# Pair sums on VectorE ahead of the norms' column sums, another order of the first loads, and a low part ahead of the bias row

## Chip, cores and metric

The kernel runs on one core of one Trainium2 chip. The metric is the device time of one execution in microseconds (us). TensorE is called PE, VectorE DVE, ScalarE ACT, GpSimd POOL, and SyncE, which here only issues loads, SP.

## What is computed

Two transformer blocks run one after the other on 256 tokens of width 1024, all in float32. The first has an attention mixer with a short convolution and a gated feed-forward part; the second adds 16 meta tokens in front (272 tokens), mixes by a convolution and a linear recurrence, and ends in a layer of 16384 experts, of which each token picks some. The change touches only the norms and the start:

```python
def rms_norm(x, g):
    xf = x.astype(jnp.float32)
    y = xf * lax.rsqrt(jnp.mean(xf * xf, axis=-1, keepdims=True) + RMS_EPS)
    return (y * g.astype(jnp.float32)).astype(x.dtype)

# first_block
h = rms_norm(x, norm_mix_pre[l]);  u = h @ w_in[l]             # norm 0
x = x + rms_norm(y, norm_mix_post[l])                          # norm 1
h = rms_norm(x, norm_ffn_pre[l])                               # norm 2
x = x + rms_norm(y, norm_ffn_post[l])                          # norm 3
# second_block
z = rmsnorm(h, g_mix[l]) @ w_in[l]                             # norm 4, 272 tokens
h = h + peer_ffn(rmsnorm(h, g_ffn[l]), ...)                    # norm 5
```

The attention adds a bias that depends on distance; its rows are made from `rel_bias` by one matrix product, the bias row.

## The kernel before

Activations lie transposed: the 1024 channels are 8 chunks (`KD`) of 128 partitions, the tokens are columns. A weight tile is 128 x 1024 numbers (512 KB), and the kernel streams 424 of them through `ring`, three slots. A product in float32 precision is made of three matmuls: each weight tile is split into a high part `w_hi` (ACT, `split_high`) and a low part `w_lo` (`split_low`: DVE for slots 0 and 1, POOL for slot 2), each activation into `x_hi` (ACT) and `x_lo` (DVE). `project` (L681) then runs 8 x 3 matmuls of 256 or 272 columns for a tile. The order on each engine is written out by hand, and semaphores join the engines. SP loads tile n when the low part of tile n-3 is there (`load_tile`, `low_wait`), so a low part frees a ring slot.

A norm has this order. ACT squares the input in four pairs of chunks into `sq` (`norm_act`, L2129; L2278 for norm 3). PE sums over the channels: one matmul with a matrix of ones for each of the 8 chunks, accumulated in PSUM (`norm_row`, L664, in the trace two records for each matmul). DVE scales and adds epsilon (L1405), ACT takes the root (L2133), DVE the reciprocal (L1408). A norm ahead of a projection goes on with 8 multiplications on DVE (L1414), the high parts on ACT (L2141) and the low parts on DVE (L1427). A norm behind one (1 and 3) scales y in pairs (L1440) and adds it to `hx1` (L1449); norms 2 and 4 square that sum pair by pair as it comes out.

At the start, SP issues the inputs x, the meta tokens, the constants `kept` (with the ones), `first` (constants of later use, with the one-hot matrix of the bias row), `rel`, and then weight tiles. PE first makes the bias row (L703), which needs `first` and `rel`, and then norm 0's sums. DVE copies the bias row out (L1454), and POOL writes it to memory and reads it back spread over 128 partitions (`bias_up`, 1.5 MB, L605); PE needs that at `bias_flip(0)`, after the fourteenth tile of the first projection. The projection starts when DVE raises `in1_even` (L1461).

Of the kernel before, what the change touches and what calls it, by code (L numbers as in the profile page):

```python
# [30 lines left out]
KD = D // P  # L31
TX = 256
N_META = 16
T2 = TX + N_META
TW = KD * P
RING = 3
BODY = 6
# [30 lines left out]
ALU = mybir.AluOpType  # L68
# [58 lines left out]
def bass_transformer_pair(nc, x_t, meta_t, kept, first, second, rel, w1_in, w1_cmp, w1_out, w1_ffn,  # L127
# [3 lines left out]
    with ExitStack() as ctx:  # L131
# [3 lines left out]
        def sem(name):  # L135
            return ctx.enter_context(nc.semaphore(name))
# [6 lines left out]
        hx = sb("hx", [P, KD, T2])  # L143
# [4 lines left out]
        sq = sb("sq", [P, KD, T2])  # L148
# [86 lines left out]
        norm_squares = sem("norm_squares")  # L235
        norm_sums = sem("norm_sums")
# [313 lines left out]
        def _(sp):  # L550
            sp.dma_start(hx1, x_t).then_inc(x_loaded, 16)
            sp.dma_start(hx[:, :, 0:N_META], meta_t).then_inc(meta_loaded, 16)
            sp.dma_start(kept_sb[:], kept).then_inc(param_loaded, 16)
            sp.dma_start(first_sb, first).then_inc(first_loaded, 16)
            sp.dma_start(oh_tab[0:32, :], rel).then_inc(rel_loaded, 16)

            def load_tile(src, n, t, i=None):
                if n >= RING:
                    low_wait(sp, n - RING, i)
                sp.dma_start(ring[:, n % RING, :], src[t]).then_inc(tile_landed[n % RING], 16)  # L560

            for (src, count), b in zip(stream, base):
# [4 lines left out]
                if b == 0:  # L567
                    for t in range(BODY):
                        load_tile(src, t, t)
                    sp.dma_start(second_sb, second).then_inc(second_loaded, 16)  # L570
                    for t in range(BODY, Z1):
                        load_tile(src, t, t)
                        if t % 2 == 0 and t < BODY + 16:
                            j = (t - BODY) // 2
                            sp.dma_start(cmp_w[:, j, :], w1_cmp[j]).then_inc(cmp_loaded, 16)
                    t0 = Z1
# [18 lines left out]
        def _(pool):  # L595
# [3 lines left out]

            pool.wait_ge(brow_ready, 1)  # L600
# [18 lines left out]
            pool_splits(0, B_IN2 + 2)  # L619
# [41 lines left out]
        def _(pe):  # L661
# [7 lines left out]
            def norm_pe(n, width, bank):  # L669
                for k in range(KD):  # L670
                    norm_row(n, k, width, bank)

# [26 lines left out]
            pe.wait_ge(param_loaded, 16)  # L699
            pe.wait_ge(first_loaded, 16)  # L700
# [4 lines left out]


            norm_pe(0, TX, 6)
# [180 lines left out]
            norm_pe(2, TX, 0)  # L888
# [27 lines left out]
            norm_pe(4, T2, 1)  # L916
# [379 lines left out]
            for m in range(16):  # L1296
                slot = tile_split(pe, B_Q + m)
                if m >= BODY:
                    pe.wait_ge(q_copied, m - BODY + 1)
                project(slot, psum[:, m % BODY, 0:TX], TX, first=None if m else X_RAW5).then_inc(tiles_used, 1)  # L1300
                if m == 1:
                    norm_pe(5, TX, 7)
# [90 lines left out]
        def _(dve):  # L1393
# [15 lines left out]

            def norm_pre(n, src, width, bank, gain, done=norm_part):  # L1410
# [19 lines left out]
            def low_norm(s, width):  # L1430
                low_x(s, lambda q: sq[:, 2 * q:2 * q + 2, 0:width])
# [20 lines left out]

            dve.wait_ge(brow_sum, 1)
            dve.tensor_copy(brow[0:N_HEADS, :], psum[0:N_HEADS, 7, :]).then_inc(brow_ready, 1)  # L1454
            dve.wait_ge(param_loaded, 16)
            dve.wait_ge(x_loaded, 16)
            split_low(dve, 0)
            split_low(dve, 1)
            norm_pre(0, hx1, TX, 6, "mix_pre")
            low_norm(X_NORM0, TX)  # L1460
# [118 lines left out]
            norm_post(1, y1, lambda q: y1[:, 2 * q:2 * q + 2, :], TX, 4, "mix_post")  # L1579
            norm_pre(2, hx1, TX, 0, "ffn_pre")  # L1580
# [41 lines left out]
            split_low(dve, B_FFN + 3 * NF + 1)  # L1622
            norm_post(3, y1, ffn_y, TX, 0, "ffn_post")
            dve.tensor_scalar(stay, colv("mu"), -1.0, 1.0, ALU.mult, ALU.add)

            norm_pre(4, hx, T2, 1, "mix2")
# [497 lines left out]
        def _(act):  # L2124
# [23 lines left out]
            split_high(act, 0)  # L2148
            split_high(act, 1)
            norm_root_act(0, TX)  # L2150
# [482 lines left out]
```

## Time and profile before

| | us |
|---|---|
| median of 3 runs | 1609.29 |
| lowest and highest | 1606.79 and 1611.38 |
| the profiled execution's own time | 1603.75 |
| its span, first to last instruction | 1602.0 |
| mean granted clock of PE in it | 0.978 of full |

The profile covers one execution. A group of rows gives start and duration in us from the start of the span, the engine, the line, the operation with the tile written and those read, and the count; what stands in brackets is how long the engine was idle before, and what ended that. The chain of work follows back from the last instruction what each step waited for. In a table of stretches, PEclk is the clock granted to PE, 1.00 being 2.4 GHz and 0.50 being 1.2 GHz.

### The profile page before, as it was taken

The numbers are of one execution on the slowest core, as the hardware profiler recorded it, in microseconds if no ns is written. First come the engines' busy times: TensorE is split into PE (matmuls) and PEld (weight loads), VectorE is DVE, ScalarE is ACT, GpSimd is POOL, SyncE is SP. The second block draws the span as 40 slices with busy tenths as digits, with TensorE's granted clock in tenths as the row PEclk, the third lists the DMA queues.
The fourth block names the chain that finished last, engine by engine and source line by source line (L and its number), as shares of the span: only waits on it lengthen the run. The fifth ranks groups of instructions, "written<-read, shape, count | busy, mean of one in ns | idle before, by whom it ended". The sixth has DMA issues, their size and how long they took to land.

```text
span 1602.0 us, 32178 instructions
## 1 busy us (share of the span) xinstructions
PE 1507.7 (94%) x11588; PEld 1380.9 (86%) x11588; DVE 1082.2 (68%) x1790; ACT 825.8 (52%) x1426; POOL 376.2 (23%) x166
## 2 busy tenths in 40 slices
PE   5998879999789999889999999999999999999998
PEld 4976669999678989889999999999999888888886
DVE  3426457778568988674678997999998544454444
ACT  3335445555455422354466556776665444444444
POOL 1210112222112301012233234221212222222221
PEclk9998999999889999999999999999999999999999
DMA  6630226555324500054645555444444566666664
GB/s 237 234 109 25 66 67 183 180 186 183 106 81 143 164 10 28 15 169 161 184 145 171 182 184 182 148 133 142 138 138 131 183 185 184 194 185 186 184 192 144
DMA packets 66231, 234.86 MB, mean 147 GB/s; under 512 B 8200, under 2 KB 9240, under 8 KB 66160
## 3 DMA queue, kind: packets, MB, share of 16 engines
q1 hardware_dynamic: 65760, 232.31, 45.9%
q0 software_dynamic: 400, 1.59, 0.3%
q8 instruction: 46, 0.75, 0.2%
q14 instruction: 25, 0.20, 0.0%
HBM read 232.80 MB, written 1.06 MB: 146 GB/s over the span
## 4 chain that ended last, share of the span: by engine, by line
PE 72%; DVE 15%; ACT 6%; issue 5%; POOL 1%; DMA 1%; DVEq 0%; SPq 0%; ACTq 0%; POOLq 0%
PE psum L681 35%; PE psum L1372 22%; PE psum L1338 4%; DVE big L1611 3%; DVE w_lo L523 3%; ACT w_hi L509 2%; DVE big L1601 2%; PE psum L1031 2%; DVE big L1651 2%; PE psum L664 1%; ACT big L2187 1%; PE psum L981 1%; PE psum L739 1%; PE psum L1022 1%; PE psum L853 1%
## 5 line engine op out<-in xcount | busy, mean ns | idle before, releaser
L681 PE MATMUL psum<-x_hi,w_hi 128*128 128x256 f32 (+1 forms) x2152 | 624.9, 290 | 39.2 <-DVE x_lo L1427 13.2
L523 POOL TENSOR_TENSOR w_lo<-ring,w_hi 128x1024 fp32r<-128x1024 f32 x141 | 352.7, 2501 | 1117.0 <-ACT w_hi L509 1117.0
L681 PE MATMUL psum<-x_lo,w_hi 128*128 128x256 f32 (+1 forms) x2152 | 613.8, 285 | 0.0
L681 PE MATMUL psum<-x_hi,w_lo 128*128 128x256 f32 (+1 forms) x2152 | 610.3, 284 | 0.0
L509 ACT ACTIVATE w_hi<-ring 128x1024 fp32r<-128x1024 f32 x424 | 445.5, 1051 | 92.0 <-PE psum L681 71.6
L523 DVE TENSOR_TENSOR w_lo<-ring,w_hi 128x1024 fp32r<-128x1024 f32 x283 | 352.2, 1245 | 151.1 <-ACT w_hi L509 147.4
L681 PEld LDWEIGHTS psum<-x_hi,w_hi 128*128 128x128 f32 x2152 | 410.7, 191 | 49.2 <-issue 32.0
L681 PEld LDWEIGHTS psum<-x_hi,w_lo 128*128 128x128 f32 x2152 | 413.4, 192 | 0.0
L681 PEld LDWEIGHTS psum<-x_lo,w_hi 128*128 128x128 f32 x2152 | 411.4, 191 | 1.7 <-issue 1.4
L2095 DVE TENSOR_TENSOR h_lo<-big,h_hi 128x256 fp32r<-128x256 f32 x128 | 69.1, 541 | 163.0 <-ACT h_hi L2519 163.0
L1372 PE MATMUL psum<-w_lo,h_hi 128*128 128x512 f32 x512 | 161.0, 395 | 0.0
L1372 PE MATMUL psum<-w_hi,h_lo 128*128 128x512 f32 x512 | 160.9, 395 | 0.0
L1372 PE MATMUL psum<-w_hi,h_hi 128*128 128x512 f32 x512 | 160.9, 395 | 0.0
L2519 ACT ACTIVATE h_hi<-big 128x256 fp32r (+1 forms) x128 | 53.3, 417 | 184.4 <-PE psum L1372 182.2
L1372 PEld LDWEIGHTS psum<-w_lo,h_hi 128*128 128x128 f32 x512 | 96.0, 187 | 23.6
L1372 PEld LDWEIGHTS psum<-w_hi,h_lo 128*128 128x128 f32 x512 | 96.0, 187 | 23.5
L1372 PEld LDWEIGHTS psum<-w_hi,h_hi 128*128 128x128 f32 x512 | 95.9, 187 | 23.4
L2494 ACT ACTIVATE sq<-kept_sb,sq 128x128 f32<-128x128 bf16 x256 | 83.6, 400 | 2.5 <-PE psum L1338 2.0
L1651 DVE SCALAR_TENSOR_TENSOR big<-big 128x272 f32<-128x272 f32 x120 | 70.8, 640 | 0.3
L2470 ACT ACTIVATE big<-psum 128x256 f32 (+1 forms) x68 | 26.2, 385 | 76.9 <-PE psum L681 76.8
L2503 ACT ACTIVATE psum<-psum 128x256 f32<-128x256 f32 x60 | 22.1, 368 | 66.3 <-PE psum L681 66.0
L695 PE MATMUL psum<-h_hi,w_hi 128*128 128x256 f32 x176 | 51.1, 291 | 3.5 <-DVE h_lo L1615 2.8
(315 smaller groups left out, 1738.0 us busy)
## 6 DMA issues: line engine op xcount, KB each, us to landing
ring<-experts SPq DMA_DIRECT2D x256, 512.0 KB, 3.5
ring<-w_ffn SPq DMA_DIRECT2D x66, 512.0 KB, 3.5
ring<-w_in SPq DMA_DIRECT2D x46, 512.0 KB, 3.6
ring<-w_mid SPq DMA_DIRECT2D x24, 512.0 KB, 3.5
ring<-w_out SPq DMA_DIRECT2D x16, 512.0 KB, 3.6
ring<-w_q SPq DMA_DIRECT2D x16, 512.0 KB, 3.9
big<-w_cmp SPq DMA_DIRECT2D x8, 512.0 KB, 5.1
big<-bias_rows POOLq DMA_DIRECT2D x1, 1536.0 KB, 9.2
```

Of the source, the lines that this page charges most:

```text
L509: act.activation(w_hi[:, n % RING, :], ring[:, n % RING, :], ACT.Copy).then_inc(high_ready, 1)
L523: eng.tensor_tensor(w_lo[:, n % RING, :], ring[:, n % RING, :], w_hi[:, n % RING, :].bitcast(F32), ALU.subtract).then_inc(low_ready2 if n ...
L681: mm = pe.matmul(dst, w[:, slot, k * P:(k + 1) * P], x[:, k, t0:t0 + width], start=(n == 0), stop=(n == 3 * len(chunks) - 1))
L695: mm = pe.matmul(psum[:, 4 + m // 2, (m % 2) * TX:(m % 2 + 1) * TX], w[:, slot, m * P:(m + 1) * P], h[:, par, :], start=False, stop=False, ...
L1031: mm = pe.matmul(psum[0:nt, FULL[name][hh], c:c + r.shape[1]], gram[hh][0:nt, a, h, 0:nt], r, start=True, stop=True)
L1338: mm = pe.matmul(gate_bank(q)[:, :, t], hot_1[q % 2][:, t, :].bitcast(F32), hot_2[q % 2][:, t, :], start=True, stop=True)
L1372: mm = pe.matmul(psum[:, 4 + 2 * tt + half, :], h[:, par, tt * P:(tt + 1) * P], w[:, slot, half * 512:(half + 1) * 512], start=False, stop ...
L1611: dve.tensor_tensor(ffn_h[:, par, :], ffn_g[:, par, :], ffn_c[:, par, 1, :], ALU.mult).then_inc(ffn_whole, 1)
L1651: ins = dve.scalar_tensor_tensor(out=conv_y[:, m, :], in0=glu[:, m, t:t + T2], scalar=w, in1=conv_y[:, m, :], op0=ALU.mult, op1=ALU.add)
L2095: dve.tensor_tensor(h_lo[:, e % 2, :], act_all[:, trip(e, i, per), :], h_hi[:, e % 2, :].bitcast(F32), ALU.subtract).then_inc(coef_low, 1)
L2494: ins = act.activation(hot_2[q % 2][:, t, :], hit_2[q % 2][:, :, t], ACT.Copy, scale=chosen_t[:, 0, bass.ds(at, 1)])
L2519: act.activation(h_hi[:, e % 2, :], act_all[:, trip(e, i), :], ACT.Copy).then_inc(coef_high, 1)
```

## The change

Four things change.

- `fold_pair(n, q, width)` on DVE adds the squares of chunk 2q+1 to those of chunk 2q, and PE sums four such pairs instead of eight chunks. Norms 0 and 3 fold all four pairs; norms 2 and 4 fold only pairs 2 and 3, and keep four single chunks. Norms 1 and 5 stay as they are.
- SP loads x, `kept`, tile 0, `first`, `rel`, tiles 1 and 2, and then the meta tokens, which stood second.
- PE makes norm 0's sums before the bias row. DVE splits only tile 0 ahead of norm 0, and copies the bias row out after the low parts of x and of tile 1. ACT makes the high part of tile 1 behind norm 0's root.
- POOL makes the low part of tile 2 before it writes the bias row out.

```diff
@@ SP
             sp.dma_start(hx1, x_t).then_inc(x_loaded, 16)
-            sp.dma_start(hx[:, :, 0:N_META], meta_t).then_inc(meta_loaded, 16)
             sp.dma_start(kept_sb[:], kept).then_inc(param_loaded, 16)
-            sp.dma_start(first_sb, first).then_inc(first_loaded, 16)
-            sp.dma_start(oh_tab[0:32, :], rel).then_inc(rel_loaded, 16)
...
+            load_tile(w1_in, 0, 0)
+            sp.dma_start(first_sb, first).then_inc(first_loaded, 16)
+            sp.dma_start(oh_tab[0:32, :], rel).then_inc(rel_loaded, 16)
...
-                    for t in range(BODY):
+                    for t in range(1, BODY):
                         load_tile(src, t, t)
+                        if t == 2:
+                            sp.dma_start(hx[:, :, 0:N_META], meta_t).then_inc(meta_loaded, 16)
@@ POOL
             pool.memset(oh_tab[32:33, :], NEG).then_inc(neg_row, 1)
+            pool.wait_ge(neg_row, 1)
+            split_low(pool, 2, None, (2,))
             pool.wait_ge(brow_ready, 1)
             pool.dma_start(bias_rows, brow[0:N_HEADS, :]).then_inc(brow_stored, 16)
...
-            pool_splits(0, B_IN2 + 2)
+            pool_splits(3, B_IN2 + 2)
@@ PE
-            def norm_pe(n, width, bank):
-                for k in range(KD):
+            def norm_pe(n, width, bank, rows=0):
+                for k in range(rows):
                     norm_row(n, k, width, bank)
+                for q in range(rows // 2, 4):
+                    pe.wait_ge(norm_folded, FOLDED[n] + q - rows // 2 + 1)
+                    mm = pe.matmul(psum[:, bank, 0:width], const("ones"), sq[:, 2 * q, 0:width], start=(q == 0), stop=(q == 3))
+                    if q == 3:
+                        mm.then_inc(norm_sums, 1)
...
             pe.wait_ge(param_loaded, 16)
+            norm_pe(0, TX, 6)
             pe.wait_ge(first_loaded, 16)
...
-            norm_pe(0, TX, 6)
...
-            norm_pe(2, TX, 0)
+            norm_pe(2, TX, 0, 4)
...
-            norm_pe(4, T2, 1)
+            norm_pe(4, T2, 1, 4)
...
-                    norm_pe(5, TX, 7)
+                    norm_pe(5, TX, 7, 8)
@@ DVE
+            def fold_pair(n, q, width):
+                dve.wait_ge(norm_squares, KD * n + 2 * q + 2)
+                dve.tensor_tensor(sq[:, 2 * q, 0:width], sq[:, 2 * q, 0:width], sq[:, 2 * q + 1, 0:width],
+                                  ALU.add).then_inc(norm_folded, 1)
...
+            for q in range(4):
+                fold_pair(0, q, TX)
+            split_low(dve, 0)
+            dve.wait_ge(param_loaded, 16)
+            dve.wait_ge(x_loaded, 16)
+            norm_pre(0, hx1, TX, 6, "mix_pre")
+            low_norm(X_NORM0, TX)
+            split_low(dve, 1)
             dve.wait_ge(brow_sum, 1)
             dve.tensor_copy(brow[0:N_HEADS, :], psum[0:N_HEADS, 7, :]).then_inc(brow_ready, 1)
-            dve.wait_ge(param_loaded, 16)
-            dve.wait_ge(x_loaded, 16)
-            split_low(dve, 0)
-            split_low(dve, 1)
-            norm_pre(0, hx1, TX, 6, "mix_pre")
-            low_norm(X_NORM0, TX)
             dve.sem_inc(in1_even, 3)
...
+            for q in range(4):
+                fold_pair(3, q, TX)
             norm_post(3, y1, ffn_y, TX, 0, "ffn_post")
@@ ACT
             split_high(act, 0)
+            norm_root_act(0, TX)
             split_high(act, 1)
-            norm_root_act(0, TX)
             high_norm(X_NORM0, 0, TX)
```

The folds of norms 2 and 4 stand as `for q in (2, 3): fold_pair(n, q, width)` right before their `norm_pre`. The rows below show the order on two engines. In brackets stand the semaphores that a row waits for.

PE at the start of the program, before: `psum<-big` is the bias row, `psum<-sq,kept_sb` a sum of squares, and L681 the first projection.

```order
L660 UNCONDITIONAL_BRANCH [waits barrier_Pool_Activation_PE_DVE_SP_release]
L703 MATMUL psum<-big 8x512 [waits rel_loaded,neg_row,first_loaded,param_loaded]
L664 MATMUL psum<-sq,kept_sb 128x256 [waits norm_squares] x8
L771 UNCONDITIONAL_BRANCH
L771 ISA
L711 ISA [waits low_ready]
L681 MATMUL psum<-x_hi,w_hi 128x256 [waits x_split,in1_even]
```

PE at the same place of the change, where L693 is the projection.

```order
L667 UNCONDITIONAL_BRANCH [waits barrier_Pool_Activation_PE_DVE_SP_release]
L681 MATMUL psum<-sq,kept_sb 128x256 [waits norm_folded,param_loaded]
L681 MATMUL psum<-sq,kept_sb 128x256 [waits norm_folded] x3
L716 MATMUL psum<-big 8x512 [waits neg_row,rel_loaded,first_loaded]
L781 UNCONDITIONAL_BRANCH
L781 ISA
L721 ISA [waits low_ready]
L693 MATMUL psum<-x_hi,w_hi 128x256 [waits x_split,in1_even]
```

The eight sums became four, wait for the folds, and stand ahead of the bias row.

DVE at the start, before: the copy of the bias row, two low parts of weights, the norm, the low parts of x.

```order
L1454 COPY big<-psum 8x512 [waits brow_sum]
L523 TENSOR_TENSOR w_lo<-ring,w_hi 128x1024 [waits high_ready,x_loaded,param_loaded]
L523 TENSOR_TENSOR w_lo<-ring,w_hi 128x1024 [waits high_ready]
L1405 TENSOR_SCALAR rms<-psum 128x256 [waits norm_sums]
L1408 RECIPROCAL rms<-rms 128x256 [waits norm_root]
L1414 SCALAR_TENSOR_TENSOR sq<-hx,kept_sb,rms 128x256 [waits dve_step]
L1414 SCALAR_TENSOR_TENSOR sq<-hx,kept_sb,rms 128x256 x7
L1427 TENSOR_TENSOR x_lo<-sq,x_hi 128x2x256 [waits high_part] x4
```

DVE at the same place of the change, with the folds (L1422) first.

```order
L1422 TENSOR_TENSOR sq<-sq 128x256 [waits norm_squares] x4
L525 TENSOR_TENSOR w_lo<-ring,w_hi 128x1024 [waits high_ready]
L1415 TENSOR_SCALAR rms<-psum 128x256 [waits norm_sums,x_loaded,param_loaded]
L1418 RECIPROCAL rms<-rms 128x256 [waits norm_root]
L1429 SCALAR_TENSOR_TENSOR sq<-hx,kept_sb,rms 128x256 [waits dve_step]
L1429 SCALAR_TENSOR_TENSOR sq<-hx,kept_sb,rms 128x256 x7
L1442 TENSOR_TENSOR x_lo<-sq,x_hi 128x2x256 [waits high_part] x4
L525 TENSOR_TENSOR w_lo<-ring,w_hi 128x1024 [waits high_ready]
L1477 COPY big<-psum 8x512 [waits brow_sum]
```

The second low part and the copy moved behind the low parts of x, and both stand ahead of the `sem_inc` of `in1_even`, which is no row of its own.

## Rows read from the trace of the kernel before

**Rows 1.** The page: span, and busy time of PE with its share.

```profile
span 1602.0 us, 32178 instructions
PE   1507.7 (94%) x11588; PEld 1380.9 (86%) x11588; DVE 1082.2 (68%) x1790; ACT 825.8 (52%) x1426; POOL 376.2 (23%) x166
```

**Rows 2.** Chain of work, 0 to 120 us: start, duration, what.

```profile
4.32 6.29 DMA big<-rel
...
10.85 1.86 PE psum L703 x2
12.71 5.17 PE psum L664 x16
...
24.64 39.45 PE psum L681 x312
```

**Rows 3.** Timeline, 0 to 75 us, rows of several engines.

```profile
2.17 1.63 SPq L553 DMA_DIRECT2D kept_sb<-kept  x1
...
8.28 2.19 ACT L2129 ACTIVATE sq<-hx 128x512 f32<-128x512 f32 x4
...
11.73 1.06 ACT L509 ACTIVATE w_hi<-ring 128x1024 fp32r<-128x1024 f32 x1 [1.26 <-DMA ring<-w_in]
...
13.36 2.34 DVE L523 TENSOR_TENSOR w_lo<-ring,w_hi 128x1024 fp32r<-128x1024 f32 x2
...
14.09 1.28 ACT L2133 ACT_TABLE_LOAD   x1
...
17.91 0.42 DVE L1405 TENSOR_SCALAR rms<-psum 128x256 f32<-128x256 f32 x1 [2.21 <-PE psum L664]
...
23.78 2.49 DVE L1427 TENSOR_TENSOR x_lo<-sq,x_hi 128x512 fp32r<-128x512 f32 x4
...
24.64 0.58 PE L681 MATMUL psum<-x_hi,w_hi 128*128 128x256 f32 x1 [6.77 <-DVEq L1461]
...
25.55 2.94 POOL L523 TENSOR_TENSOR w_lo<-ring,w_hi 128x1024 fp32r<-128x1024 f32 x1 [8.61 <-ACT w_hi L509]
```

**Rows 4.** Single microseconds: length, busy time by engine, PEclk, DMA share, GB/s.

```profile
22.00:23.00 1.00, 0.00 (x0) 0.00 (x0) 1.00 (x4) 0.78 (x2) 0.00 (x0) 0.78 0.97 359
29.00:30.00 1.00, 1.00 (x9) 1.00 (x8) 0.00 (x0) 0.11 (x1) 0.00 (x0) 0.81 0.46 74
432.00:433.00 1.00, 0.01 (x1) 0.02 (x1) 1.00 (x3) 0.66 (x1) 0.00 (x0) 0.58 0.00 0
438.00:439.00 1.00, 1.00 (x3) 0.68 (x3) 0.00 (x0) 0.00 (x0) 0.00 (x0) 0.51 0.00 0
```

**Rows 5.** Loads by line: KB each, us from issue to landing.

```profile
big<-bias_rows POOLq DMA_DIRECT2D x1, 1536.0 KB, 9.2
hx<-x_t SPq DMA_DIRECT2D x1, 1024.0 KB, 6.2
...
kept_sb<-kept SPq DMA_DIRECT2D x1, 539.0 KB, 6.5
```

**Rows 6.** Timeline: the load of tile 7 (first of two), and its high part.

```profile
35.45 4.02 SPq L560 DMA_DIRECT2D ring<-w_in  x2
41.30 1.06 ACT L509 ACTIVATE w_hi<-ring 128x1024 fp32r<-128x1024 f32 x1 [1.43 <-PE psum L681]
```

**Rows 7.** Timeline of norm 2's last sums and last squares.

```profile
216.87 1.99 PE L664 MATMUL psum<-sq,kept_sb 128*128 128x256 f32 x8 [0.26 <-ACT sq L2129]
216.97 0.63 ACT L2129 ACTIVATE sq<-hx 128x512 f32<-128x512 f32 x1 [0.16 <-DVE hx L1449]
```

**Rows 8.** Timeline from the last feed-forward step through norms 3 and 4.

```profile
417.71 0.43 DVE L1615 TENSOR_TENSOR h_lo<-big,h_hi 128x256 fp32r<-128x256 f32 x1 [0.48 <-ACT h_hi L2268]
...
422.98 2.06 ACT L2278 ACTIVATE sq<-psum 128x512 f32<-128x512 f32 x4 [4.35 <-PE psum L695]
423.63 3.72 PE L664 MATMUL psum<-sq,kept_sb 128*128 128x256 f32 x16 [0.75 <-ACT sq L2278]
...
432.99 6.88 PE L664 MATMUL psum<-sq,kept_sb 128*128 128x272 f32 x16 [5.63 <-ACT sq L2129]
...
435.04 1.45 ACT L2129 ACTIVATE sq<-hx 128x544 f32<-128x544 f32 x2 [0.73 <-DVE hx L1449]
```

More of the change, by code:

```diff
@@ L235, in bass_transformer_pair @@
         norm_squares = sem("norm_squares")
+        norm_folded = sem("norm_folded")
+        FOLDED = {0: 0, 2: 4, 3: 6, 4: 10}
         norm_sums = sem("norm_sums")
@@ L1579, in _ @@
             norm_post(1, y1, lambda q: y1[:, 2 * q:2 * q + 2, :], TX, 4, "mix_post")
+            for q in (2, 3):
+                fold_pair(2, q, TX)
             norm_pre(2, hx1, TX, 0, "ffn_pre")
@@ L1622, in _ @@
             split_low(dve, B_FFN + 3 * NF + 1)
+            for q in range(4):
+                fold_pair(3, q, TX)
             norm_post(3, y1, ffn_y, TX, 0, "ffn_post")
             dve.tensor_scalar(stay, colv("mu"), -1.0, 1.0, ALU.mult, ALU.add)
+            for q in (2, 3):
+                fold_pair(4, q, T2)
             norm_pre(4, hx, T2, 1, "mix2")
```

## The prediction

> **What bounds the kernel now.** I read the page first. PE is busy 94% of a span of 1602.0 us [rows 1], so what a change can win outside the matmuls is small. The question is which stretches have PE short of work, and what the chain runs through there. The chain of work from 0 to 120 us shows the first: it waits for the load of `rel` until 10.61, then takes 1.86 us for the bias row, 5.17 us for norm 0's sums, and reaches the projection at 24.64 [rows 2]. From there on PE is the chain for 39 us. So whatever comes earlier ahead of 24.64 moves everything behind it. The timeline of the same stretch shows what stood ready: ACT had squared x by 10.47 (8.28 + 2.19), while the sums began only at 12.7 and the scaling at 17.91 [rows 3]. In norms 3 and 4 the sums are again a piece of the chain in which everything else waits (3.72 and 6.88 us), and in norm 2 their last part (1.99 us) [rows 7, 8].
>
> **What one sum costs.** The clock comes first. Norm 2's last four matmuls took 1.99 us, norm 3's eight 3.72 us [rows 7, 8]: (3.72 - 1.99)/4 = 0.43 us each, and 1.99 - 4 x 0.43 = 0.27 us of tail. PEclk was full in both. At 1.2 GHz I take twice the spacing, 0.86, and a tail of 0.4 (estimate); norm 4's eight in 6.88 us, at 1.2 GHz until just before 439 [rows 4, 8], and the bias row's 512 columns in 1.86 us [rows 2] agree with it. A fold is a DVE addition of 128x256 f32. None of this form is in the trace; the nearest is the subtraction of 128x256 at L1615, 0.43 us [rows 8]. As a bound from above, a quarter of the 1024 columns of L523, whose two took 2.34 us, is 0.29, so the fixed part is already in 0.43; the range is 0.3 to 0.5, and I take 0.43 and 0.05 for each handover.
>
> **Norm 0.** The squares stay at 8.28 to 10.47, a pair each 0.55 us, since the load of x stays first. Folds then end at about 9.35, 9.9, 10.4 and 10.95. PE needs `kept` too, which landed at 2.17 + 6.5 = 8.7 [rows 3, 5] and now stands a place further ahead. PE starts cold at 9.4, so its four sums come every 0.86 us, more slowly than the folds: 9.4 + 4 x 0.86 + 0.4 = 13.25. Before, scaling began at 17.91 [rows 3]. That is 4.65 us earlier. Three things could be later than 13.25. DVE splits tile 0 ahead of the scaling: tile 0 was the sixth load and its high part began at 11.73; now it is third, ahead of 690 KB of `first`. At the 1024 KB + 539 KB landed by 8.7, 512 KB more at the same pace is 9.7 to 10.5, so ACT starts on it when it is done with the squares at 10.5, ends at 11.55 (1.06), DVE at 12.75 (2.34/2) [rows 3]. ACT's table load of 1.28 us then fits in 11.6 to 12.9. If the tile lands as late as before, DVE ends at 14.0 and 0.75 us of gain is lost. The bias row now follows the sums at 13.3 to 15.1, off the chain.
>
> **From scaling to projection** it was 24.64 - 17.91 = 6.73 us [rows 3], and the same instructions follow. ACT's high part of tile 1 (1.06 us) goes into ACT's idle time between root and the first `x_hi`, during DVE's reciprocal and first multiplications. New is that a low part of 1.2 us and the bias row's copy of 0.7 us stand ahead of the `sem_inc` that lets PE go. In the trace PE was let go at 24.6 by DVE's sequencer while the last low parts of x ran until 26.27 [rows 3]: the increment passes work that is only queued. So I price this at 0.1 us for two more instructions to issue. If the increment had to wait until the copy is done, it would cost 26.27 + 1.2 + 0.7 - 24.6 = 3.6 us; that is the upper bound. The Trainium skill (TensorE: Matmul & The Clock Gate, its opening table) gives ScalarE, VectorE and GpSimdE queues that hold 8 instructions, strictly in order. By it the five queued here (three low parts of x, one of the tile, the copy) fit; no row shows five. I keep 0.1. The low part of tile 1 ends at 22.8, the second tile's matmuls start near 25 (24.64 + 4.8 - 4.55): hidden. Tile 2's low part on POOL keeps its place behind ACT (25.55 before, near 21 now [rows 3]); the DMA pair of the bias row goes behind it. Norm 0's term is 4.65 - 0.1 = **4.55 us**.
>
> **Norm 2.** The last squares end at 217.60 (216.97 + 0.63), the sums at 218.86 [rows 7]. With folds the last one ends at 218.08, its sum at 218.12 + 0.70 = 218.82. That is **0.0 us** (bounds -0.3 to 0.2): the two matmuls saved are paid by a fold in the chain.
>
> **Norm 3.** Squares start at 422.98 and end at 425.04, one each 0.49 us [rows 8]. DVE is idle. The last fold ends at 425.51, the last sum at 425.56 + 0.70 = 426.26, against 427.35. That is **1.1 us** (bounds 0.9 to 1.3).
>
> **Norm 4.** PE starts at 432.99 at 1.2 GHz and is the bound, since the squares are there at 436.49 (435.04 + 1.45) [rows 8]. Now it has four chunks and two pairs of 272 columns, 0.91 each: 6 x 0.91 + 0.4 = 5.85 us; the folds (last by 437.0) are in time for the fifth and sixth, which start at 436.6 and 437.5. Against 6.88 that is **1.0 us**. Had the clock been low throughout, eight took 7.7 and the gain were 1.85; had it been full, the last sum hangs on the last square and the gain is 0.
>
> **Sum.** 4.55 + 0.0 + 1.1 + 1.0 = 6.65, say 6.7 us. Span 1602.0 becomes 1595.3, the profiled execution's 1603.75 becomes 1597.1. This execution lies 5.5 us under the median of the runs, so the median becomes 1609.3 - 6.7 = 1602.6. What follows norm 4 is unchanged. A run of this kernel can tell about 0.3% (4.8 us) from no change, so the forecast lies only 1.9 us beyond that.
>
> **Rivals.**
> - *The clock is still up when the projection starts* (chance 0.12). Before, PE was idle from 17.88 to 24.64, the clock fell in the second from 22 (0.78, so about 4.7 us in), and the projection ran at 1.2 GHz until about 29.4 [rows 4]. Ahead of norm 4 it fell at 432.16, 4.8 us after norm 3's sums. Now PE works until 15.1 and starts again near 20.1, an idle of 5.0 us instead of 6.8. Should the clock rise in 9.4 to 15.1 and hold, the first 24 matmuls come each 0.12 instead of 0.21 us: up to 2.3 us more, a gain of 9.0, 1600.3 us. The Trainium skill (same page, "HAM oscillation") has the clock fall after a gap without matmuls, so a shorter gap speaks for this rival; the trace agrees with the rule, falling in both gaps above, but the cooler, shorter work ahead of the gap speaks against it.
> - *The gate of the projection, or a late tile 0* (0.14). The increment waits for part of the queue (up to 3.6 us), or the first tile costs 0.75. The gain is 3 to 5.5: 1604 to 1606.3 us.
> - *The spread bias rows meet the tile stream* (0.12). Their 1.5 MB took 9.2 us [rows 5] in a quiet time from 16 to 25; now they are issued near 26.5, when tiles 6 and 7 and other loads of 512 KB are under way. Tile 7 was issued at 35.45 and its high part needed it at 41.30 [rows 6], 5.8 us for a load that takes about 4 alone. 1.5 MB at 400 GB/s is 3.9 us of traffic. Two tiles late by 2 us cost at most some 3 us, and ACT makes high parts ahead of need: the gain is 3.5 to 6, 1603.3 to 1605.8.
> - *Slower* (0.04). By the same mechanism: if the spread load's packets keep the stream waiting for its whole 9.2 us and again in the next slots. A stall beyond 6.7 us turns the sign, 11.5 us gives slower by 0.3% (1614). It decides from the point where tile 7 lands more than 6.7 us after PE could use it; its slack makes that unlikely.
> - *The change doesn't do what it says* (0.05): norm 0's chain is set by another wait, for instance the folds or `kept`, and gains under 3 us: 1605 to 1607.5.
>
> **How the numbers follow.** The forecast has 0.53 and its own range 1601 to 1604.5. The range 1599 to 1606.5 takes in the warm clock below and most of the gate, tile stream and norm 4 at full clock above. Faster by over 0.3% (under 1604.5): 0.49 of the forecast, 0.12 of the first rival and 0.07 of the next two, 0.68 in all. Slower 0.04, and 0.28 between.
>
> **What would show it.** In the new profile: the first sum near 9.4 and scaling near 13.3; the projection 6.8 us behind, let go by DVE's sequencer; no ACT high part waiting for `ring` from 25 to 45; norm 3's scaling 4.4 us behind its first square before, 3.3 now; norm 4's sums of some 5.9 us at 1.2 GHz. Wrong would make it a scaling in norm 0 that waits for the low part of tile 0 or for a slow load, a projection that starts after the copy of the bias row, or clock phases that fall otherwise.

## The result, and the profile after

The changed kernel takes 1594.43 us (median of 4 runs, 1593.44 to 1597.27), the kernel before beside it 1608.04 (4 runs, 1604.76 to 1611.38): a ratio of 0.9922 with a 95% interval of 0.9901 to 0.9943, so faster by 12.5 us (by the medians 13.6). The forecast was 6.7 us. The profiled execution of the changed kernel took 1597.27 us, its span is 1595.2; before it was 1603.75 and 1602.0. **Between the two traces lie 6.8 us, as forecast; between the runs lie 12.5 to 13.6.** That difference is what the experiments are about. The agreement of the traces with the forecast is in part luck, as the leads at the end of this section show.

The page of the changed kernel, span and busy time:

```profile
span 1595.2 us, 32113 instructions
PE 1508.6 (95%) x11564; PEld 1380.9 (87%) x11564; DVE 1087.6 (68%) x1802; ACT 826.0 (52%) x1426; POOL 376.9 (24%) x166
```

The chain of work of the changed kernel at its start (start, us, what), to be held against [rows 2]:

```profile
0.75 5.72 DMA hx<-x_t
...
8.49 0.44 DVE sq L1422
...
9.07 3.77 PE psum L681 x8
...
19.72 39.67 PE psum L693 x312
```

The load of `rel` and the bias row are gone from the chain; it goes from x by its squares and one fold to the sums. The projection's first thirteen tiles run without a pause again (39.67 us for 312 matmuls, 39.45 before [rows 2]), so no load stalls them. The timeline of the same stretch, against [rows 3]:

```profile
7.83 2.19 ACT L2152 ACTIVATE sq<-hx 128x512 f32<-128x512 f32 x4
8.49 1.99 DVE L1422 TENSOR_TENSOR sq<-sq 128x256 f32<-128x256 f32 x4 [8.49 <-ACT sq L2152]
9.07 3.75 PE L681 MATMUL psum<-sq,kept_sb 128*128 128x256 f32 x8 [9.07 <-DVE sq L1422]
9.93 1.04 ACT L511 ACTIVATE w_hi<-ring 128x1024 fp32r<-128x1024 f32 x1
...
11.00 1.23 DVE L525 TENSOR_TENSOR w_lo<-ring,w_hi 128x1024 fp32r<-128x1024 f32 x1 [0.52 <-ACT w_hi L511]
...
12.75 1.87 PE L716 MATMUL psum<-big 33*8 33x512 f32 x2
12.97 0.42 DVE L1415 TENSOR_SCALAR rms<-psum 128x256 f32<-128x256 f32 x1 [0.74 <-PE psum L681]
...
18.84 2.49 DVE L1442 TENSOR_TENSOR x_lo<-sq,x_hi 128x512 fp32r<-128x512 f32 x4
...
19.72 0.58 PE L693 MATMUL psum<-x_hi,w_hi 128*128 128x256 f32 x1 [5.09 <-DVEq L1478]
...
20.69 4.02 POOL L525 TENSOR_TENSOR w_lo<-ring,w_hi 128x1024 fp32r<-128x1024 f32 x1 [19.58 <-ACT w_hi L511]
...
21.25 1.22 DVE L525 TENSOR_TENSOR w_lo<-ring,w_hi 128x1024 fp32r<-128x1024 f32 x1
...
22.39 0.67 DVE L1477 COPY big<-psum 8x512 f32<-8x512 f32 x1
...
24.99 0.28 PE L693 MATMUL psum<-x_hi,w_hi 128*128 128x256 f32 x1
25.10 0.28 PE L693 MATMUL psum<-x_lo,w_hi 128*128 128x256 f32 x1
...
29.11 0.94 POOL L612 DMA_DIRECT2D big<-bias_rows  x1 [3.76 <-DMA bias_rows<-big]
```

PE waits for DVE's first fold of two squares (8.49) and sums from 9.07 on, at 1.2 GHz. Norm 0's scaling stands at 12.97 instead of 17.91 and the projection 6.75 us behind it at 19.72 instead of 24.64: 4.92 us earlier. It starts while the low part of tile 1 and the copy of the bias row (22.39) are still queued on DVE. Its matmuls start 0.2 us apart until 24.99 and 0.12 apart from then: full clock comes 5.3 us into the projection. Two things took longer and cost nothing: POOL's low part (4.02 us, 2.94 before [rows 3]) and its wait for the stored bias rows (3.76).

Norms 3 and 4 of the changed kernel, against [rows 8]:

```profile
420.42 2.07 ACT L2301 ACTIVATE sq<-psum 128x512 f32<-128x512 f32 x4 [5.21 <-PE psum L707]
421.05 1.89 DVE L1422 TENSOR_TENSOR sq<-sq 128x256 f32<-128x256 f32 x4 [4.59 <-ACT sq L2301]
421.53 2.17 PE L681 MATMUL psum<-sq,kept_sb 128*128 128x256 f32 x8 [1.21 <-DVE sq L1422]
...
429.33 3.99 PE L671 MATMUL psum<-sq,kept_sb 128*128 128x272 f32 x8 [5.63 <-ACT sq L2152]
...
433.12 1.79 PE L681 MATMUL psum<-sq,kept_sb 128*128 128x272 f32 x4
```

Last, the places at which each kernel scales in norms 1 to 4, and three high parts of weight tiles that both make (number 25, 133 and 421 of the 424). The kernel before, on its timeline:

```profile
116.58 1.04 ACT L509 ACTIVATE w_hi<-ring 128x1024 fp32r<-128x1024 f32 x1
...
208.18 0.42 DVE L1405 TENSOR_SCALAR rms<-psum 128x256 f32<-128x256 f32 x1 [1.59 <-PE psum L664]
...
218.90 0.42 DVE L1405 TENSOR_SCALAR rms<-psum 128x256 f32<-128x256 f32 x1 [2.02 <-PE psum L664]
...
427.39 0.42 DVE L1405 TENSOR_SCALAR rms<-psum 128x256 f32<-128x256 f32 x1 [7.50 <-PE psum L664]
...
439.90 0.44 DVE L1405 TENSOR_SCALAR rms<-psum 128x272 f32<-128x272 f32 x1 [4.08 <-PE psum L664]
...
649.82 1.05 ACT L509 ACTIVATE w_hi<-ring 128x1024 fp32r<-128x1024 f32 x1
...
1577.63 1.04 ACT L509 ACTIVATE w_hi<-ring 128x1024 fp32r<-128x1024 f32 x1
```

The changed kernel:

```profile
110.30 1.04 ACT L511 ACTIVATE w_hi<-ring 128x1024 fp32r<-128x1024 f32 x1
...
205.63 0.42 DVE L1415 TENSOR_SCALAR rms<-psum 128x256 f32<-128x256 f32 x1 [1.59 <-PE psum L671]
...
216.30 0.42 DVE L1415 TENSOR_SCALAR rms<-psum 128x256 f32<-128x256 f32 x1 [0.79 <-PE psum L681]
...
423.74 0.42 DVE L1415 TENSOR_SCALAR rms<-psum 128x256 f32<-128x256 f32 x1 [0.79 <-PE psum L681]
...
434.95 0.44 DVE L1415 TENSOR_SCALAR rms<-psum 128x272 f32<-128x272 f32 x1 [1.64 <-PE psum L681]
...
640.08 1.05 ACT L511 ACTIVATE w_hi<-ring 128x1024 fp32r<-128x1024 f32 x1
...
1570.87 1.04 ACT L511 ACTIVATE w_hi<-ring 128x1024 fp32r<-128x1024 f32 x1
```

The lead of the changed kernel is 4.9 us at the projection, 6.3 at the 25th tile, 2.6 at norms 1 and 2, 3.7 at norm 3, 5.0 at norm 4, 9.7 at the 133rd tile and 6.8 at the end. Only three of these steps lie where instructions differ: the start (4.9), norm 3 (1.1) and norm 4 (1.3), 7.3 us in all. The other steps, where the instructions are the same, are -2.4 us up to norm 1, 4.8 between norm 4 and the 133rd tile and -3.0 from there to the 421st. They nearly cancel in this pair of traces, and so the two traces come out 6.8 us apart. Between 110 and 208, and from 450 to 720, the same instructions run in the same order, and the lead moves by 3.0 to 4.8 us at a time. The tables of stretches (length, busy us of PE, PEld, DVE, ACT, POOL, then PEclk, DMA share and GB/s) say with what. Before, then changed:

```profile
116.00:200.00 84.00, 70.74 (x410) 52.95 (x411) 48.91 (x105) 45.52 (x143) 4.78 (x2) 0.92 0.14 44
600.00:660.00 60.00, 55.85 (x1023) 52.76 (x1022) 47.29 (x92) 16.34 (x35) 6.27 (x2) 0.94 0.06 20
660.00:735.00 75.00, 66.28 (x628) 62.58 (x623) 49.93 (x69) 35.35 (x45) 14.53 (x6) 1.00 0.41 133
```

```profile
116.00:200.00 84.00, 74.48 (x385) 56.73 (x385) 44.90 (x97) 43.95 (x141) 5.18 (x3) 0.84 0.14 42
600.00:660.00 60.00, 56.60 (x1035) 53.53 (x1032) 47.72 (x97) 16.48 (x35) 6.27 (x2) 1.00 0.04 11
660.00:735.00 75.00, 66.55 (x508) 63.55 (x508) 46.27 (x56) 36.10 (x45) 15.93 (x7) 0.93 0.48 154
```

In the attention stage (116 to 200), where PE waits for ACT and DVE again and again, the changed kernel's execution had a mean clock of 0.84 against 0.92; around 600 to 660 it is the other way round (1.00 against 0.94), and from 660 the other way again. So a single trace holds some microseconds that belong to where the clock stood in that one execution; the stretch behind norm 4 is compared over all traces at the end of the experiments.

### The profile page after: what moved, and what is told of

Same layout as the page of the kernel before. It is cut to its first block, busy times and chain, and to the rows that moved or that the text cites. A ratio compares the mean times of both kernels' runs of the same rounds, so it can differ in the third digit from the quotient of the medians.

```text
span 1595.2 us, 32113 instructions
## 1 busy us (share of the span) xinstructions
PE 1508.6 (95%) x11564; PEld 1380.9 (87%) x11564; DVE 1087.6 (68%) x1802; ACT 826.0 (52%) x1426; POOL 376.9 (24%) x166
## 4 chain that ended last, share of the span: by engine, by line
PE 73%; DVE 16%; ACT 5%; issue 5%; POOL 1%; DMA 0%; DVEq 0%; ACTq 0%; POOLq 0%
PE psum L693 36%; PE psum L1382 22%; PE psum L1348 4%; DVE big L1630 3%; DVE w_lo L525 3%; DVE big L1674 2%; ACT w_hi L511 2%; DVE big L1620 2%; PE psum L1041 1%; PE psum L749 1%; PE psum L991 1%; PE psum L863 1%; PE psum L671 1%; DVE sq L1429 1%; POOL w_lo L525 1%
## 5 line engine op out<-in xcount | busy, mean ns | idle before, releaser
L693 PE MATMUL psum<-x_hi,w_hi 128*128 128x256 f32 (+1 forms) x2152 | 627.1, 291 | 37.4 <-DVE x_lo L1442 12.9
L693 PE MATMUL psum<-x_lo,w_hi 128*128 128x256 f32 (+1 forms) x2152 | 615.8, 286 | 0.0
L693 PE MATMUL psum<-x_hi,w_lo 128*128 128x256 f32 (+1 forms) x2152 | 612.2, 284 | 0.0
L693 PEld LDWEIGHTS psum<-x_hi,w_hi 128*128 128x128 f32 x2152 | 412.7, 192 | 48.9 <-issue 31.7
L693 PEld LDWEIGHTS psum<-x_hi,w_lo 128*128 128x128 f32 x2152 | 415.6, 193 | 0.0
L693 PEld LDWEIGHTS psum<-x_lo,w_hi 128*128 128x128 f32 x2152 | 413.7, 192 | 1.7 <-issue 1.4
```

The source lines that it names most:

```text
L693: mm = pe.matmul(dst, w[:, slot, k * P:(k + 1) * P], x[:, k, t0:t0 + width], start=(n == 0), stop=(n == 3 * len(chunks) - 1))
```

## The experiments

All gains are given by the ratio to the kernel before on the same chip, times 1607 us; ranges are the 95% intervals. The theory at the start: the chain loses 6.8 us, and the rest of the 12.5 is PE's clock, which the two traced executions do not represent. The rivals: one part of the change is worth more than its chain shows, or the medians were a chance. The chain's worth of a part is what its traces win at the projection and in the norms.

**One part at a time.** The whole change again, the start alone (`norm_pe(2|3|4, ..., 8)` and the folds of norms 2 to 4 out), the pair sums of norms 2 to 4 alone (norm 0, order and loads as before), and the kernel before once more.

> The whole change once more, for a second trace and more runs. Theory A (the sum holds, and the profiled execution of before was a lucky one while the rest of the 13.6 us is chance of where the clock falls): over more runs the gain comes down to 7 to 9 us. Theory B (something beyond the shortened chain pieces gains in every run): the gain stays at 12 to 14 us, and the same pieces of the chain are 6 us shorter than in the trace of before in a place that the sum did not name. Both expect scaling in norm 0 near 13.0 and the projection near 19.7.

> Only the start of the change (loads, norm 0 with pair sums ahead of the bias row, tile 2's low part first); norms 2, 3 and 4 sum eight chunks as before. Theory A: 4.9 us faster than before, as the projection starts 4.9 us earlier. Theory B, if the unnamed gain belongs to the start: 10 to 12 us faster.

> Only the pair sums of norms 2, 3 and 4, with the start as before. Theory A: 2.4 us faster (0, 1.1 and 1.3 us). Theory B, if the unnamed gain belongs to the folds: 7 to 9 us faster. If both halves gain as Theory A says but the whole gains 13, the two parts act on each other.

> The kernel before, unchanged, for a second trace of it and as a test of what the comparison tells from nothing. Both theories: a ratio of 1.000 within 0.002. Theory A expects its trace to have the same length as the first trace in all stretches in which the clock is up, and other lengths only where PE works at 1.2 GHz; its span then is 1602 plus what it spends more at 1.2 GHz. Theory B expects a stretch in which it is longer at full clock too.

Measured: the whole 12.9 us (10.9 to 14.9; 1594.27 us, 5 runs), the start 7.7 (5.1 to 10.3), the pair sums 5.6 (3.9 to 7.4), the kernel before -0.5 (-1.9 to 1.0). The gain is no chance: the 7 to 9 us of Theory A for the whole did not come. The parts add up (13.3), and each is worth more than its chain, 4.9 and 2.4, and less than Theory B gave it. Within one kernel the time goes with PE's mean granted clock: of the six runs of the start alone, 1595.49 and 1595.58 us stand at 0.982, 1603.60 and 1606.46 at 0.974. The second trace of the kernel before (1604.84 us) takes 208.45 us from norm 2's scaling to norm 3's for 208.49 in the first; elsewhere it has other low stretches and other lengths, as Theory A expected. The trace of the second execution of the whole change shows how much the clock moves for one and the same program:

```profile
12.50 1.02 PE L716 MATMUL psum<-big 33*8 33x512 f32 x2
19.46 0.58 PE L693 MATMUL psum<-x_hi,w_hi 128*128 128x256 f32 x1 [5.94 <-DVEq L1478]
...
22.57 0.28 PE L693 MATMUL psum<-x_hi,w_lo 128*128 128x256 f32 x1
...
116.00:200.00 84.00, 74.43 (x365) 55.58 (x364) 43.58 (x92) 40.81 (x130) 4.76 (x2) 0.80 0.11 38
```

The bias row took 1.02 us instead of 1.87, full clock came 3.1 us into the projection instead of 5.3, and then the attention stage ran at 0.80: it reached that stage 2.0 us ahead of the first execution (108.01 and 110.04), and norm 1 2.1 us behind it (207.70 and 205.63).

**The clock held up.** In both kernels PE gets idle matmuls in its gaps, on a bank that nobody reads: 11 ahead of the projections of norms 0, 2 and 4, 5 ahead of the last `ffn_down` and 9 between norms 3 and 4.

```diff
+            def fill_gap(norm, part, bank):
+                filler(4, bank)
+                pe.wait_ge(norm_root, norm + 1)
+                filler(3, bank)
+                for q, n in enumerate((2, 1, 1)):
+                    pe.wait_ge(norm_part, 4 * part + q + 1)
+                    filler(n, bank)
```

> The kernel before with idle matmuls (zeros times constants, 0.43 us each at 2.4 GHz, into a bank nobody reads) in PE's gaps: 11 each between the sums and the projection in norms 0, 2 and 4, 9 between norms 3 and 4, 5 ahead of the last down tile. The output is not touched. Theory C (the gain beyond the traced one is the clock: in most executions norms 3 and 4 meet PE at 1.2 GHz, where eight sums cost twice): the clock stays up through the gaps, the projections start at 2.4 GHz, and this kernel is 5 to 9 us faster than before. Theory D (the surplus is not the clock): little changes, -3 to +3 us.

> The whole change with the same idle matmuls. Against the run of the kernel before with them, Theory C expects only the shortened chain at full clock: 4.9 us at the start, 1.1 in norm 3, nothing in norms 2 and 4, 6 us in all. Theory D expects the full 12.6 us between these two as well. If the clock is what costs, this is also the fastest kernel: 1585 to 1591 us.

Measured: 1591.11 us (5 runs) for the kernel before with them, 14.6 us faster (12.5 to 16.7) for 5 to 9 expected, and 1588.10 (5 runs) for the changed one, 16.1 faster (13.5 to 18.6). **With the clock held up the change is worth 3.0 us by the medians and 1.4 by the ratios**, not 12.5, though the projection still starts 5.0 us earlier (24.87 and 19.86). Two of the changed kernel's five runs stand apart (1593.95 and 1592.19 us, clock 0.981 and 0.983; the others 1586.09 to 1588.10 at 0.986 to 0.988), so this worth is known to some 4 us either way: it is less than 12.5, and not clearly less than the chain's 6. Norm 4 and the start of the projection, of the kernel before with idle matmuls:

```profile
24.87 0.39 PE L681 MATMUL psum<-x_hi,w_hi 128*128 128x256 f32 x1 [0.82 <-DVEq L1482]
...
428.92 2.10 PE L664 MATMUL psum<-sq,kept_sb 128*128 128x272 f32 x8 [0.20 <-ACT sq L2150]
...
116.00:200.00 84.00, 74.36 (x399) 56.51 (x398) 46.18 (x99) 44.24 (x141) 5.65 (x3) 0.86 0.14 48
```

and of the changed kernel with them:

```profile
19.86 0.39 PE L693 MATMUL psum<-x_hi,w_hi 128*128 128x256 f32 x1 [0.83 <-DVEq L1499]
20.08 0.28 PE L693 MATMUL psum<-x_lo,w_hi 128*128 128x256 f32 x1
...
427.01 1.52 PE L681 MATMUL psum<-sq,kept_sb 128*128 128x272 f32 x4 [0.68 <-DVE sq L1443]
...
116.00:200.00 84.00, 74.88 (x391) 57.28 (x391) 43.50 (x92) 42.92 (x135) 6.84 (x3) 0.84 0.15 45
```

The projection now starts at full clock (0.12 us from the second matmul on). Norm 4's sums hang on the last square in both, end at 431.02 (428.92 + 2.10) and 428.53 (427.01 + 1.52), and nothing is gained there: from the first sum (426.16 and 423.78) it is 4.86 and 4.75 us. Norm 3's pair sums win there what they won without: the lead is 1.2 us at norm 2, 2.4 at norm 3, 2.5 at norm 4 and 2.8 at the end. The attention stage, which has no idle matmuls, stays at 0.84 to 0.86.

The granted clock says how the 14.6 us come about. In the stretches that it gives as 1.2 GHz, PE worked 53.7 and 64.0 us in the two traces of the kernel before, and 32.1 us with the idle matmuls. Work at 1.2 GHz takes twice as long, so 22 to 32 us less of it should give 11 to 16 us (an estimate). The two traces of the changed kernel have 60.0 and 64.6 us of it, 35.6 with the idle matmuls: over the whole execution they show no better clock than the kernel before.

**The parts with the clock held up.** The start alone and the pair sums alone, with the same idle matmuls.

> The start alone (loads, order, pair sums of norm 0), with the idle matmuls that hold the clock up ahead of the projections. The kernel before with the same idle matmuls took 1591.1 us, the whole change with them 1588.1. Theory A (the surplus of the start over its 4.9 us of chain is the clock in and around the gaps): the start gains at most its chain, 3 to 5 us, 1586 to 1588. Theory B (the start's 7.7 us belong to the part itself, whatever the clock does): 1583.5. Theory C (the attention stage takes back part of any earlier start, as the two traces with idle matmuls show): 1588 to 1589.5.

> The pair sums of norms 2, 3 and 4 alone, with the same idle matmuls; against 1591.1 us for the kernel before with them. Theory A: with the clock up, norm 2 gives 0, norm 3 1.1 us as without them and norm 4 some 0.4, since its last sum hangs on the last square: 1589.5. Theory B (the folds' 5.6 us belong to them whatever the clock does): 1585.5. Theory C (nothing here is behind the attention stage, so it takes nothing back): as A.

Measured: 1589.52 us (6 runs), 16.9 faster than before (12.9 to 20.7), and 1593.61 (6 runs), 14.9 (11.4 to 18.5). Against the filled kernel before (14.6) the start is worth 2.2 us and the pair sums 0.3, where they were worth 7.7 and 5.6. Each comparison has 4 us or more to either side, so no single one is firm; all three stand at or under their chain, and none shows its surplus. Theory A is nearest for both parts, and Theory C (the attention stage takes part back) fits the start as well.

**More idle matmuls**, 23 in the attention stage too:

> The whole change with the idle matmuls of before and 23 more in the attention stage: 10, 2 and 7 ahead of the first three turns of the probabilities, into the bank that the turn then overwrites, and 4 ahead of the output projection. In the traces that stage took 71 to 81 us, the same matmuls at other clocks. If it is the clock, the stage takes 71 us or less, the spread of the runs shrinks, and the time falls below the filled kernel's 1588.1, to 1580 to 1586. If the stage's length has another cause, the time stays or rises by the 10 us of matmuls put in.

Measured 1589.49 us (5 runs), 17.5 faster (15.4 to 19.6). The clock of 116 to 200 rises to 0.94, but from the 25th tile to norm 1's scaling it takes 95.4 us as before (95.2 with the idle matmuls in the norms alone), and the kernel is not faster. The 1580 to 1586 us of the clock's theory did not come. That the idle matmuls stand in the way of real ones would explain both; it was not measured by itself.

**The start taken apart.** The new order without pair sums in any norm, and the whole change with the old order of loads:

> Only the order of the start: loads, norm 0 ahead of the bias row, tile 2's low part first; norm 0 sums eight chunks, and so do norms 2 to 4. Eight sums from about 8.6 us on, mostly at 0.86 us each, end near 15.2 to 15.6. By the chain it gains 2.3 to 2.8 us in its trace, and the pair sums of norm 0 are worth the other 2.2. Theory D, with the surplus in the order of the loads: it gains 5 us or more.

> The whole change but the order of the loads, which is that of before (meta tokens second, the constants of later use and rel ahead of tile 0). Tile 0's high part then starts at 11.7 as before, its low part ends near 14.0, and scaling in norm 0 waits for it: 1.0 us slower than the whole change. If the surplus lies in the loads (Theory D), it is 4 us slower or more.

Measured: the order alone 2.7 us (1.0 to 4.3; 12 runs), for a projection 3.8 us earlier (20.88), where 2.3 to 2.8 were expected; the whole change with the old loads 8.5 (6.1 to 11.1), for a projection at 20.68. So by the chain the order, loads included, gives 3.8 us, the folds of norm 0 some 1.1 more, and the loads 1.0 of all this. The times part it otherwise: norm 0's folds are worth 5.0 us (7.7 for the start less 2.7), and the loads 4.4 (12.9 less 8.5), which meets the 4 us at which Theory D put the surplus into the loads; but the order alone, with the new loads, stays under the 5 us that the same theory asked of it. Each of these differences has about 3 us to either side.

**Delays.** One, two and three needless additions of 1.1 us each on DVE, between norm 0's multiplications and the low parts of x, in the changed kernel and then in the one before; and norm 3's pair sums alone. The first of the additions:

```diff
             norm_pre(0, hx1, TX, 6, "mix_pre")
+            dve.tensor_tensor(conv_m, hx1[:, 0:4, :], hx1[:, 4:8, :], ALU.add)
             low_norm(X_NORM0, TX)
```

> The whole change with one needless DVE addition of 128x1024 (about 1.13 us) into an unused region, between norm 0's multiplications and the low parts of x, so that everything from the first projection on comes 1.1 us later. Theory E (the untraced surplus is where the clock's falls meet the attention stage, and that place is nearly the same in each execution): the time changes by something else than 1.1 us, between -4 and +8 us. Theory F (the clock falls at random places, so only the mean over executions counts): 1.1 us slower than the whole change, within the noise of 1 us: 1595.4.

> The same with two such additions, 2.3 us. Theory E: a change that is not 2.3 us, and not twice that of one addition. Theory F: 2.3 us slower than the whole change, 1596.5.

> The same with three, 3.4 us. Theory E: back near the whole change plus 3.4 us, 1597.7, with one or both of the other two off the line between. Theory F: 1597.7 as well, with the other two on the line.

> The kernel before with one needless DVE addition (1.1 us) between norm 0's multiplications and the low parts of x. Theory G (most executions of the kernel before fall at an unlucky place of the clock, and any shift helps): less than 1.1 us slower, or faster, by as much as 4 us. Theory H (its place is an ordinary one and the surplus is won wherever the start lies): 1.1 us slower.

> The same with two additions, 2.3 us. Theory G: up to 4 us better than the 2.3 us slower of Theory H.

> The same with three additions, 3.4 us. Theory H: 3.4 us slower. Theory G: about the same here, as the place comes round again.

> The kernel before with the pair sums of norm 3 alone. By the trace, at 2.4 GHz, they win 1.1 us. If norm 3's sums meet 1.2 GHz in part of the executions, where four matmuls fewer are 3 us, and norm 4's start moves as well, it is 2 to 3.5 us.

| us | projection starts | median | gain by ratio |
|---|---|---|---|
| changed, no delay | 19.72 and 19.46 | 1594.27 | 12.9 |
| changed, 1, 2, 3 delays | 20.81, 21.89, 22.77 | 1594.35, 1595.96, 1596.68 | 13.0, 11.9, 8.4 |
| before, no delay | 24.64 and 25.29 | 1607.41 | -0.5 |
| before, 1, 2, 3 delays | 25.73, 27.45, 28.00 | 1611.16, 1606.76, 1610.72 | -3.2, -0.5, -2.7 |
| before, norm 3's pair sums | 25.56 | 1604.35 | 1.9 |

The changed kernel keeps its surplus when its start is delayed: at 22.77 it is 1.9 us ahead of the kernel before at the projection, and still 8.4 faster (5.0 to 11.7). In the kernel before the same delays cost 3.2 us (0.5 to 5.9), 0.5 (-2.2 to 3.4) and 2.7 (0.2 to 5.3) for 1.1, 2.3 and 3.4. These ranges hold the length of the delay in all three, and the changed kernel's times lie within some 1.5 us of its own line, so Theories F and H, a cost of the delay and no more, fit all six. Theory E's place of the clock that nearly every execution meets is not seen, nor an unlucky place of the kernel before that any shift would leave (Theory G): none of its delayed versions is clearly faster. Norm 3's four pair sums (eight records) took 2.17 us as in the changed kernel, which should give 1.1, and gave 1.9 (-0.5 to 4.3), which fits that and the 2 to 3.5 expected.

**Where the surplus of the pair sums lies.** From norm 4's scaling to the high part of the 133rd tile every kernel runs the same instructions, but for the idle matmuls where a kernel has them. Read in the trace of every run:

| norm 4's scaling to the 133rd tile | traces | us | mean | PEclk |
|---|---|---|---|---|
| norm 4 sums eight chunks (before, twice; the start alone; the order alone; before with 1, 2, 3 delays) | 7 | 208.8 to 209.9 | 209.3 | 0.96, one 0.97 |
| pair sums in norms 3 and 4 (changed, twice; the pair sums alone; old loads; changed with 1, 2, 3 delays) | 7 | 204.9 to 207.2 | 205.9 | 0.97 to 0.98 |
| pair sums in norm 3 alone | 1 | 206.9 | 206.9 | 0.98 |
| with idle matmuls, whatever the sums | 5 | 203.6 to 205.4 | 204.2 | 0.98 to 0.99 |

The stretch in the first trace of the kernel before (length, busy us of PE, PEclk, DMA share, GB/s):

```profile
439.90:649.82 209.92, 189.79 (x2332) 0.96 0.26 82
```

and in the first trace of the changed kernel:

```profile
434.95:640.08 205.13, 187.14 (x2332) 0.98 0.26 83
```

The two groups of seven do not overlap. The pair sums win 3.4 us here in the mean, behind the place where their instructions end. All of it lies in the last 96 us, from the high part of the 130th tile on, and there it goes with the clock: the first group has 6.8 us at 1.2 GHz in every trace and takes 95.7 to 97.1 us; the second has 3.4 us of it in four traces (93.4 to 94.4 us) and none in three (91.9 to 92.1). With idle matmuls the same holds whatever the sums (92.0 us with none, 93.3 twice with 3.4, 94.6 and 95.1 with 6.8), and the pair sums win nothing there. With 0.05 us in norm 2, 1.1 in norm 3 and 1.3 in norm 4 (12.1 us from norm 3's scaling to norm 4's in the mean of the one group, 10.8 in the other) that makes 5.8 us, for 5.6 measured. The start has no such stretch: from the projection to norm 1's scaling the eight traces with the new start took 183.2 to 190.1 us (mean 186.7), the seven with the old one 181.8 to 189.4 (184.2).

## Why the prediction was wrong

**The chain was right, term by term.** Norm 0: scaling 4.94 us earlier for 4.65 forecast, since PE could start at 9.07, not 9.4. The increment passed the queued low part and copy: 6.75 us from scaling to projection for 6.73 before, so the gate cost 0.02 for 0.1. Tile 0 was split by 12.23 (11.00 + 1.23), ahead of the scaling. Norm 2: 0.05 for 0.0 (2.60 less 2.55). Norm 3: 1.1 for 1.1, the scaling 3.32 us behind the first square for 4.41. Norm 4: sums from 429.33 to 434.91, 5.58 us for 5.85, a gain of 1.3 for 1.0, with PE at 1.2 GHz until 434.6. No tile was late, so the rivals of the gate, the spread load and the change that does nothing are out, and with them the slower case. The clock was not up at the start of the projection in this trace, nor in any other of the changed kernel without idle matmuls; with them it was. In the second trace of the change the clock was up from 12.3 but fell at 15.7, 2.2 us after PE's last matmul there, so the first rival's rise came and did not hold.

**The steps that failed** are two. The first is "What follows norm 4 is unchanged". The instructions are, but not their time: from norm 4's scaling to the 133rd tile the pair sums win 3.4 us in the mean of seven traces against seven (4.8 in the first pair), at a PEclk of 0.97 to 0.98 for 0.96. The prediction took the clock as a given of each gap ("PEclk was full in both", norm 4 at 1.2 GHz "until just before 439") and put at nothing what another gap does to the clock behind it.

The second is "This execution lies 5.5 us under the median of the runs, so the median becomes 1609.3 - 6.7". It carries the difference of two single executions over to the medians. The profiled execution of the kernel before took 1603.75 us, less than any of the runs that it was then compared by (1604.76 to 1611.38), 4.3 us under their median of 1608.04; the one of the changed kernel took 1597.27, more than every other (1593.44 to 1594.70), 2.8 us above its median. With the 6.5 us between the two times that is the 13.6 of the medians. The second execution profiled of the whole change was again the slowest of its five (1596.98). That the traces gave the forecast's 6.8 us all the same is luck: in the first pair the 4.8 us behind norm 4 were taken back by 2.4 ahead of norm 1 and 3.0 behind the 133rd tile. The 5.5 us between trace and median, which the prediction noted, were the sign that the trace was no middle one, and the range should have had them on its low side.

**What stands in its place.** For the pair sums it is shown that PE's clock carries their surplus: it lies in a stretch of equal instructions, goes there with the time at 1.2 GHz, and is gone where both kernels have idle matmuls. For the whole the idle matmuls speak for the same: they make the kernel before 14.6 us faster with its own order of work kept, and with them the change is worth 1.4 to 3.0 us instead of 12.5. The prediction priced no part of the 14.6 us as movable. The clock may also be why less than the chain's 5.0 us remains with the idle matmuls: from the row at which the attention stage starts on ACT (111.35 and 108.53) to norm 1's scaling (205.16 and 203.97) the changed kernel took 95.44 us, the other 93.81, and of the 5.0 us at the projection 1.2 were left at norm 1 in those two traces.

**What stays open** is the start's surplus and the reason for the clock's course. The start is worth 7.7 us (5.1 to 10.3) for a chain of 4.9, which is hardly beyond the noise; its traces show no stretch that wins it, and the order, the loads and norm 0's folds each have differences of 3 us to either side. Nor does the clock of whole executions tell: the mean granted clock of the changed kernel's runs is 0.975 and 0.976, that of the kernel before 0.975 (19 runs), and 0.988 and 0.985 for the two with idle matmuls (none of these counts the first low stretch of a program, see the last section). So the words "a better clock" are shown for the stretch behind norm 4, and for the start they are not. Why shorter sums in norms 3 and 4 leave less time at 1.2 GHz so far behind them no run tells.

**The fastest** are the kernels with idle matmuls: 1588.1 us (the whole change), 1589.5 (with more of them) and 1589.5 (the start alone). They can't be told apart, and all beat both kernels without them.

## What to carry to other kernels

Read the chain for what a change does, but where PE waits often, ask how the traced execution stands to the other runs before carrying its difference over: here one trace was 5.5 us under the median, and equal instructions moved the lead between 2.6 and 9.7 us. Where the clock falls in the gaps, try idle matmuls in them first: 18 lines on PE gave 14.6 us, as much as or more than a change of order, loads and sums on five engines (12.5). Take the traces of all runs together, not in pairs: a stretch of equal instructions behind the change held 3.4 us that no chain piece of the change showed. Gains of chain and clock do not add: 12.5 and 14.6 apart, 16.1 together.

## What was not expected of the hardware

The attention stage runs the same instructions in 91.9 us (before, 116.31 to 208.18), 95.6 (changed, 110.04 to 205.63) or 99.7 (changed, second execution, 108.01 to 207.70) between the same two places, with mean clocks of 0.92, 0.84 and 0.80.

The PEclk of a table of stretches does not show the first low stretch of a program. In the changed kernel:

```profile
20.00:24.00 4.00, 4.00 (x20) 4.00 (x21) 3.06 (x5) 0.54 (x1) 3.31 (x1) 1.00 0.11 20
```

It says 1.00, while matmuls of 256 columns started 0.21 us apart, as at 1.2 GHz, and 0.12 apart from 24.99 on. At the start, go by the spacing.

POOL's low part of 1024 columns, 2.94 us before [rows 3] and 2.39 later in the changed kernel, took 4.02 at 20.69, beside DVE's low parts; why it took longer there is not shown.
